# Attention whose probabilities are divided by row on GpSimd and turned by a transpose, with neighbourhood values in matmuls of 512 columns

## The reference, cut to what matters

```python
# kind A: every query sees all 1024 keys; 8 query heads share 2 key/value heads
sc = jnp.einsum('bqkgd,bskd->bkgqs', qi, k).astype(jnp.float32) * scale
p = jax.nn.softmax(sc, axis=-1)
o = jnp.einsum('bkgqs,bskd->bqkgd', p, v)
# kind B: tokens form a grid of 16 rows x 64 columns; a query sees 8 rows x 16 columns
r0 = jnp.clip(r - kh // 2, 0, rows - kh)
sc = jnp.where(mask, sc + bias, -jnp.inf)     # learned bias by relative position
p = jax.nn.softmax(sc, axis=(-2, -1))
o = jnp.einsum('bhjqkc,bkjchd->bjqhd', p, v_band)
```

## Time and profile before

| | |
|---|---|
| median of 3 runs | 2989.11 us (2982.98 to 2990.6) |
| span of the profiled execution, first to last instruction | 2980.2 us; its own time is not recorded apart from the span |
| TensorE busy | 2780.2 us, 93% |
| VectorE / ScalarE / GpSimd busy | 1447.7 / 923.2 / 161.8 us |
| mean granted TensorE clock | 0.965 |
| attention, kind A | about 2376 to 2633 us of the span |
| attention, kind B | about 2633 to 2862 us of the span |

### The profile page before, as it was taken

The page is one execution under the profiler, slowest core; times in us unless marked ns, Lnnn a source line. Parts: engine busy times, 40 slices in busy tenths (PEclk is TensorE's granted clock), DMA queues, the critical chain, the costliest instruction groups (busy, mean ns, idle before and its releaser), DMA issues.

```text
span 2980.2 us, 36559 instructions
## 1 busy us (share of the span) xinstructions
PE 2780.2 (93%) x13564; PEld 2272.1 (76%) x13564; DVE 1447.7 (49%) x2275; ACT 923.2 (31%) x1437; POOL 161.8 (5%) x128
## 2 busy tenths in 40 slices
PE   8989999999997999989999999999999999988988
PEld 2467777777776988867787787777788888877876
DVE  3764444454436144244434334345412188877753
ACT  3342222222123222242222222223212266654531
POOL 2100000000002000100000000000100000022111
PEclk9999999999998998999999999999999999999888
DMA  8522222222102600221111111102434522233311
GB/s 301 184 67 80 93 84 84 84 84 85 57 15 81 177 8 21 93 99 56 43 42 43 56 42 42 42 0 106 122 114 143 134 58 65 81 92 102 84 71 57
DMA packets 179482, 245.34 MB, mean 82 GB/s; under 512 B 55728, under 2 KB 136752, under 8 KB 179376
## 3 DMA queue, kind: packets, MB, share of 16 engines
q1 hardware_dynamic: 156944, 208.52, 21.6%
q10 hardware_dynamic: 22432, 35.40, 4.4%
HBM read 210.33 MB, written 39.58 MB: 84 GB/s over the span
## 4 chain that ended last, share of the span: by engine, by line
PE 79%; issue 7%; DVE 7%; ACT 4%; DMA 1%; POOL 1%; ACTq 1%; DVEq 0%; SPq 0%; POOLq 0%
PE banks L1615 20%; PE banks L1616 19%; PE banks L1617 19%; PE banks L1961 5%; PE banks L1695 3%; PE banks L1990 2%; DVE Hlo L1286 1%; ACT Whi L842 1%; PE banks L1979 1%; PE banks L1802 1%; PE banks L1803 1%; PE banks L1804 1%; PE banks L1948 1%; DVE X L1331 1%; PE banks L1949 1%
## 5 line engine op out<-in xcount | busy, mean ns | idle before, releaser
L1615 PE MATMUL banks<-Hhi,Whi 128*128 128x512 f32 x1792 | 714.2, 399 | 17.4 <-ACT TB L964 6.7
L1616 PE MATMUL banks<-Hlo,Whi 128*128 128x512 f32 x1792 | 703.6, 393 | 0.0
L1617 PE MATMUL banks<-Hhi,Wlo 128*128 128x512 f32 x1792 | 703.3, 392 | 0.0
L1331 DVE SCALAR_TENSOR_TENSOR X<-banks,mod,X 128x512 f32<-128x512 f32 x512 | 373.4, 748 | 243.2 <-PE banks L1617 243.2
L1615 PE MATMUL banks<-Mhi,Whi 128*128 128x512 f32 x1024 | 411.4, 402 | 58.9 <-DVE X L1331 58.9
L1615 PEld LDWEIGHTS banks<-Hhi,Whi 128*128 128x128 f32 x1792 | 341.1, 190 | 97.5 <-issue 8.7
L1616 PE MATMUL banks<-Mlo,Whi 128*128 128x512 f32 x1024 | 404.9, 395 | 0.0
L1617 PE MATMUL banks<-Mhi,Wlo 128*128 128x512 f32 x1024 | 404.7, 395 | 0.0
L1616 PEld LDWEIGHTS banks<-Hlo,Whi 128*128 128x128 f32 x1792 | 340.8, 190 | 74.0 <-issue 4.2
L1617 PEld LDWEIGHTS banks<-Hhi,Wlo 128*128 128x128 f32 x1792 | 340.1, 190 | 72.0
L842 ACT ACTIVATE Whi<-stage 128x2048 fp32r<-128x2048 f32 x93 | 177.3, 1907 | 636.1 <-PE banks L1617 622.6
(11 more groups left out here) (171 smaller groups left out, 3032.4 us busy)
## 6 DMA issues: line engine op xcount, KB each, us to landing
stage<-w SPq DMA_DIRECT2D x64, 1024.0 KB, 5.6
stage<-ada_w SPq DMA_DIRECT2D x48, 1024.0 KB, 5.2
stage<-w_in SPq DMA_DIRECT2D x13, 1024.0 KB, 6.5
stage<-sgu_in SPq DMA_DIRECT2D x8, 1024.0 KB, 6.8
x_saved<-X SPq DMA_DIRECT2D x16, 512.0 KB, 2.7
X<-x_saved SPq DMA_DIRECT2D x16, 512.0 KB, 6.1
QS<-q_heads ACTq DMA_DIRECT2D x28, 256.0 KB, 3.9
KH<-k_heads ACTq DMA_DIRECT2D x28, 256.0 KB, 3.9
```

What stands on the lines that cost most here:

```text
L1331: nc.vector.scalar_tensor_tensor(out=X[:, k, half(hf)], in0=Dn[:, i % D_BANKS, :], scalar=gate[:, k:k + 1], in1=X[:, k, half(hf)], op0=ALU ...
L1615: nc.tensor.matmul(out_bank, whi, xhi, start=start, stop=False)
L1616: nc.tensor.matmul(out_bank, whi, xlo, start=False, stop=False)
L1617: return nc.tensor.matmul(out_bank, wlo, xhi, start=False, stop=stop)
```

## The change

It is confined to the attention of the second block, and has four parts.

1. The division by the row sum leaves the turn. GpSimd multiplies the row of probabilities in place by the reciprocal (`scale`, a `tensor_scalar` with the reciprocal as a per-partition scalar). VectorE no longer makes the diagonal matrix. The turn becomes `nc.tensor.transpose`, a matmul in transpose mode against the identity, and waits for `scale` instead of the diagonal.
2. The value product of kind B takes whole groups as that of kind A does: the turned probabilities are stored at their place among all key tiles, the group's six key tiles are multiplied in 512 columns, and what no query of the group sees there is zero. The zeros are written once per buffer by GpSimd (`zero_window`, `zero_pad`) since nothing overwrites them. Outputs of a group start when all four units' turned probabilities are there.
3. The mask is added to the bias table in two halves, for the first head of a pair during units 13 and 14 of the pair before, for the second head at units 4 and 5.
4. Loads are issued from SyncE's queue in the order of need, each as soon as its buffer is free, not from ScalarE's at set units.

```diff
@@ helpers @@
+    def probs_t(x, u, kind, k, m):
+        k += neighbourhood(u % QT)[0] // 2 if kind == "B" else 0
         return x[:, (u // 4) % 2, k:k + m, (u % 4) * P:(u % 4 + 1) * P]
+    def key_tiles(kind, g):
+        return range(KT) if kind == "A" else range(2 * (g % 2), 2 * (g % 2) + 6)
@@ SyncE @@
+            def attend(T, kind, i, before, last):
+                following = ("B", 0) if last else (kind, i + 1)
+                if before is not None:
+                    for what in ("q", "kh", "kl", "bias", "v"):
+                        if what in needed(kind):
+                            load_head(sync, T, kind, i, 1, what)
+                if not (last and kind == "B"):
+                    for what in ("q", "kh", "kl", "bias", "v"):
+                        if what in needed(following[0]):
+                            load_head(sync, T, *following, 0, what, ahead=1)
@@ GpSimd @@
-            def mask_bias(T, e):
-                pool.wait_ge(mask_loaded, 16)
-                pool.wait_ge(bias_loaded[e], T.loads(16, 4))
-                nc.gpsimd.tensor_tensor(bias[:, e, :], bias[:, e, :], mask[:], ALU.add).then_inc(bias_masked, 1)
+            def scale(T, u, kind):
+                pool.wait_ge(rd_done, T("v", u + 1))
+                pool.sem_inc(sums_seen, 1)
+                row = PE_[:, u % 2, 0:width(kind, u)]
+                nc.gpsimd.tensor_scalar(out=row, in0=row, scalar1=rden[:, u % 4:u % 4 + 1], scalar2=1.0,
+                                        op0=ALU.mult, op1=ALU.mult).then_inc(probs_scaled, 1)
+            def mask_bias(T, e, part, ahead=0):
+                if part == 0:
+                    pool.wait_ge(mask_loaded, 16)
+                    pool.wait_ge(bias_loaded[e], T.loads(16, 4, ahead))
+                at = slice(part * (NF + NI) // 2, (part + 1) * (NF + NI) // 2)
+                nc.gpsimd.tensor_tensor(bias[:, e, at], bias[:, e, at], mask[:, at], ALU.add).then_inc(bias_masked, 1)
+            def zero_pad(T, u):
+                reach(pool, t_ready, T("v2", 2 * u - 2))
+                nc.gpsimd.memset(PE_[:, u % 2, NI:NI + HD], 0.0).then_inc(pad_zeroed, 1)
+            def zero_window(T, g):
+                reach(pool, o_ready, T("vg", g - 1))
+                outside = (((4, 6, 0, 256), (5, 6, 256, 384), (0, 1, 384, 512)),
+                           ((2, 4, 256, 512), (7, 8, 0, 128), (2, 3, 128, 256)))[g]
+                for x in (PTh, PTl):
+                    for k0, k1, q0, q1 in outside:
+                        nc.gpsimd.memset(x[:, g, k0:k1, q0:q1].bitcast(F32), 0.0).then_inc(window_zeroed, 1)
             def attend(T, kind, i, before, last):
                 for u in range(PAIR):
-                    if kind == "B" and u in (0, 4):
-                        reach(pool, mixed_done, T("vg", u // 4 - 2))
-                        mask_bias(T, u // 4)
-                    if kind == "B" and u in (3, 7):
-                        pool.wait_ge(bias_masked, T.masked(u // 4))
+                    if u % 4 == 0:
+                        reach(pool, mixed_done, T("vg", (u - 5) // 4))
+                    for w, k in lagged(u, 2, kind, before):
+                        scale(T, w, k)
+                    if kind == "B" and before == "A" and u < 2:
+                        zero_pad(T, u)
+                    if kind == "B" and before == "A" and u in (4, 8):
+                        zero_window(T, u // 4 - 1)
+                    if kind == "B" and u in (4, 5):
+                        mask_bias(T, 1, u - 4)
+                    if (kind == "B") != last and u in (13, 14):
+                        mask_bias(T, 0, u - 13, ahead=1)
                     for w, k in lagged(u, 8, kind, before):
                         if w % 4 == 3:
+                            pool.wait_ge(probs_scaled, T("v", u - 1))
                             gated(T, w // 4, tile_of(kind, i, w < 0))
@@ VectorE, invert_sum @@
-                reach(dve, rd_done, T("v", u - 3))
-                nc.vector.reciprocal(rden[:, u % 4:u % 4 + 1], den[:, u % 4:u % 4 + 1]).then_inc(rd_own, 1)
-                dve.wait_ge(rd_own, T("v", u + 1))
-                reach(dve, t_ready, T("v2", 2 * u - 2))
-                nc.vector.tensor_scalar(out=DG[:, u % 2, :], in0=con("ident"), scalar1=rden[:, u % 4:u % 4 + 1],
-                                        scalar2=None, op0=ALU.mult).then_inc(rd_done, 1)
+                reach(dve, probs_scaled, T("v", u - 3))
+                nc.vector.reciprocal(rden[:, u % 4:u % 4 + 1], den[:, u % 4:u % 4 + 1]).then_inc(rd_done, 1)
@@ TensorE, turn @@
-                pe.wait_ge(rd_done, T("v", u + 1))
+                pe.wait_ge(probs_scaled, T("v", u + 1))
                     reach(pe, tl_done, T("v2", 2 * u + g - 1))
                     for k in range(m):
                         a = (first + k) * P
-                        part = min(P, n - a)
-                        ins = nc.tensor.matmul(TP[0:part, g, k * P:(k + 1) * P], PE_[:, u % 2, a:a + part],
-                                               DG[:, u % 2, :], start=True, stop=True)
+                        ins = nc.tensor.transpose(TP[:, g, k * P:(k + 1) * P], PE_[:, u % 2, a:a + P], con("ident"))
@@ TensorE, outputs @@
+                    pe.wait_ge(tl_done, T("v2", 8 * g + 8))
+                tiles = key_tiles(kind, g)
+                todo = [(k, x) for k in tiles for x in (PTh, PTl)]
+                n = len(todo) // 4
+                for k, x in todo[n * part_of:n * part_of + n]:
+                    ins = nc.tensor.matmul(OB[:, g % 2, :], VT[:, e, k, :], x[:, g % 2, k, :],
+                                           start=k == tiles[0] and x is PTh, stop=k == tiles[-1] and x is PTl)
```

More of the change, by code:

```diff
@@ L73 @@
          "finish").split()
-LOAD_AT = {1: "q", 2: "kh", 3: "kl", 4: "bias", 7: "v"}
 class Tally:
@@ L1084, in exp, with probs_hi @@
                                      accum_out=den[:, u % 4:u % 4 + 1]).then_inc(exp_done, 1)
-            def probs_hi(T, u, n):
-                for g, first, m in banks(n):
+            def probs_hi(T, u, kind):
+                for g, first, m in banks(width(kind, u)):
                     act.wait_ge(t_ready, T("v2", 2 * u + g + 1))
@@ L1100, in attend @@
             def attend(T, kind, i, before, last):
-                following = ("B", 0) if last else (kind, i + 1)
                 for u in range(PAIR):
                     for w, k in lagged(u, 3, kind, before):
-                        probs_hi(T, w, width(k, w))
-                    if before is not None and u in LOAD_AT and LOAD_AT[u] in needed(kind):
-                        load_head(nc.scalar, T, kind, i, 1, LOAD_AT[u])
-                    if u - QT in LOAD_AT and not (last and kind == "B") and LOAD_AT[u - QT] in needed(following[0]):
-                        load_head(nc.scalar, T, *following, 0, LOAD_AT[u - QT], ahead=1)
+                        probs_hi(T, w, k)
                     for w, k in lagged(u, 1, kind, before):
@@ L1950, in scores, with turn @@
                 ins.then_inc(s_ready, 1)
-            def turn(T, u, n):
-                pe.wait_ge(rd_done, T("v", u + 1))
-                for g, first, m in banks(n):
+            def turn(T, u, kind, zeroed=0):
+                pe.wait_ge(probs_scaled, T("v", u + 1))
+                reach(pe, pad_zeroed, zeroed)
+                for g, first, m in banks(width(kind, u)):
                     reach(pe, tl_done, T("v2", 2 * u + g - 1))
@@ L1973, in outputs @@
                     reach(pe, os_done, T("vg", g - 1))
-                if kind == "A":
-                    if part_of == 0:
-                        pe.wait_ge(tl_done, T("v2", 8 * g + 8))
-                    for k in (2 * part_of, 2 * part_of + 1):
-                        for x in (PTh, PTl):
-                            ins = nc.tensor.matmul(OB[:, g % 2, :], VT[:, e, k, :], x[:, g % 2, k, :],
-                                                   start=k == 0 and x is PTh, stop=k == QT - 1 and x is PTl)
-                else:
-                    pe.wait_ge(tl_done, T("v2", 2 * w + 2))
-                    t = part_of
-                    first, rows = neighbourhood(w % QT)
-                    n = rows * GRID
-                    tiles = (n + P - 1) // P
-                    for k in range(tiles):
-                        part = min(P, n - k * P)
-                        for x in (PTh, PTl):
-                            ins = nc.tensor.matmul(OB[:, g % 2, t * P:(t + 1) * P],
-                                                   VT[0:part, e, first // 2 + k, :],
-                                                   x[0:part, g % 2, k, t * P:(t + 1) * P],
-                                                   start=k == 0 and x is PTh, stop=k == tiles - 1 and x is PTl)
+                    pe.wait_ge(tl_done, T("v2", 8 * g + 8))
+                    reach(pe, window_zeroed, zeroed)
+                tiles = key_tiles(kind, g)
[4 more added lines that the diff above has]
```

(5 more changed lines are left out.)

40 lines of the change are left out of this document (22 added, 18 removed).

## The result

The changed kernel takes 2866.3 us in the median of 4 runs (2865.0 to 2869.0), the kernel before 2986.1 us beside it on the same chip (2980.7 to 2990.6). The ratio is 0.960, with a 95% interval of 0.9584 to 0.9617: 120 us less. The forecast was 2911 us, 78 less, in a range of 2872 to 2968. The profiled execution spans 2867.1 us (2980.2 before).

The account below looks back on a forecast made before the run. TensorE was taken to bound the attention, with VectorE right behind in A. A -37, B -50, clock +13 and tail -4 sum to -78 us: span 2902, time 2911 us, range 2872 to 2968 for 8 in 10.

Parts of the forecast that it names:

- TensorE bounds A, and a transpose is one pass at the same pace: Kind A's turn: one 0.111 us pass per transpose instead of two, so TensorE needs 2.72 us a unit, not 3.61.
- The rival of a transpose without gain: Turn on TensorE: transpose no cheaper than two passes, only the stall goes in A; about 2950 us; 8 in 100.
- the circles: Waits closing every two units: in A 3.5 us plus scale via GpSimd, 5.2 via VectorE; scale under 1.9 us is covered.
- the midpoint to the two-input row: Scale on GpSimd: half the two-input slope, 1.06 ns a column plus 0.2 us; 1.29 us in A, 0.78 in B.
- what goes and what comes at a group's end: End of four units: vanished stall of 1 us mostly taken back by 0.8 us in A, 0.7 in B.
- The stalls: VectorE's diagonal beside GpSimd's gating multiply lasts 1.30 us, not 0.29; 34 us over all 128 diagonals.
- The new wait behind the gating product: Group ends: gating multiply (1.28 us) sits before the next scale on GpSimd's queue, adding 0.8 us in A, 0.7 in B.
- the allowances for limits that lie close: Unit times: A taken at 2.9 us with TensorE at 2.72; B at 2.3 with limits near 1.8 to 1.9.
- the loads, "mostly beside waits: nothing": Load issues leaving ScalarE's queue, about 1.1 us per pair, mostly beside waits: costed at nothing.
- the clock, +13 us: Kind B: TensorE less busy, so more lower clock; a quarter of units at 3.6 us instead of 2.8, 13 us added.
- this rival's event: Clock falls to the lower level in A too, +86 us there if throughout, 3075 us; 8 in 100, half of it mild.
- Tail: After the last units: 12 matmuls of 0.43 us and a 2 us wait replace 46 small ones of 10.86 us; -4 us.

Follow-up runs that it names:

- cut gating product: Kernel before with GpSimd's gating product cut to 8 of 512 columns, leaving most of that product out: 2944.2 us, ratio 0.988.
- the one with small outputs: Changed kernel with kind B's value product again in 128 columns for each unit: 2898.8 us, ratio 0.973.

## Why the prediction was off in size, step by step

**Right: TensorE bounds A, and a transpose is one pass at the same pace.** 0.110 us for 0.111, a unit at 2.71 for 2.72. The rival of a transpose without gain is ruled out.

**Right: the circles.** The scale took 1.119 us where 1.29 were worked out, and at 512 and 576 columns 0.692 and 0.745 for 0.78: 0.83 ns a column and some 0.27 us fixed, so the memset row was its near relative, not the midpoint to the two-input row. It hides either way.
**Right: what goes and what comes at a group's end.** The stalls were computed at 34 us. The cut gating product takes out those beside it and leaves those beside the masks: the diagonals are busy 49.8 us instead of 70.7, and the time falls by 37. In A that is 0.75 us a group for a stretch of 1.0; in B, at 1.56, it brings the clock with it. The new wait behind the gating product was put at 0.8 and 0.7 us a group; moving it away gives 0.85 and 0.82.

**Wrong: the allowances for limits that lie close, 0.2 us a unit in A and 0.4 in B.** "For two limits so close I allow 0.2 and take 2.9." In the trace after there is no such jitter: TensorE's 2.71 and VectorE's 2.66 run beside each other, and a group of A takes 4 x 2.71 + 1.83 = 12.67 instead of 13.7. Over 16 groups of A that is 16 us, 12 of them the allowance and 4 the group's end, 1.8 for 2.1 (at A's start and end the steps are uneven, so A as a whole lies 15 below). In B the limits were put near 1.9 us and 2.3 was taken. In three groups at full clock (turns from 2639.88, 2650.15 and 2660.24 us on) the turns follow at 1.6 to 2.1 us, 1.9 in the mean, so the limit was right and the allowance was not there. The group's end costs some 2.5 us for 2.0. With the clock's part a group was foreseen at 11.2 + 0.8 = 12.0 and took 10.25.

These allowances and the clock below are the steps that failed. Of the 35 us between the forecast 78 and the spans' 113, 15 lie in A and 21 in B with its tail, 13 of which were put on the clock; the remaining 7 of the medians' 120 are the difference between spans and medians.

**Wrong: the loads, "mostly beside waits: nothing".** Moving them was worth 30 us in the kernel before (the end of the waits for the bias included) and, put back, they cost 32 in the kernel after. ScalarE's queue is in order, and the issues stood behind a copy and ahead of an exponential that two circles wait for: about 1.1 us each time, in view in the chain of before. This isn't a second gap in the sum: the sum builds a group from the limits of the units, in which no issue stands, so the loads' gain was in it without being named. The error lies in the reading. Had the loads stayed, half of A's allowance would have been needed: put back, they raise a group of A by 0.38 us, 0.1 a unit.

**Wrong in sign: the clock, +13 us.** The prediction read the lower level as a matter of how little TensorE does in B and expected more of it. TensorE does do less, 135 us busy in 175 after 207 in 229, yet the granted clock of B rose from 0.89 to 0.96. In the kernel before, stand in stretches that begin behind gaps; each edit that shortens gaps, the cut gating product alone or the loads alone, brings B to 1.00 with the matmuls unchanged. With the wide outputs the falls in the kernel after are over in 3.4 us; in the kernel before they held for 3.4 us twice, for 13.7 twice, and for over 14 at the end of B. So the 13 us were not there, and part of the low stretches of before went as well.

**The other rivals.** The clock did not fall in A: 1.00. With the scale doubled it does, for 3.4 us at a time behind longer idle times of TensorE, so gaps can bring this rival's event, in small. The Trainium skill's page TensorE: Matmul & The Clock Gate, Part 4, says that transpose mode doesn't count as busy. No run here bears that out for float32: 400 transposes with nothing else for 43.9 us keep 1.00. The measurement decides; the chance of 8 in 100 rested on no row.

**Tail.** Forecast -4. The step from the last but two to the last gating product fell from 19.9 to 11.0 us, -9. The chain after has 12 wide products in 3.00 us, 0.25 each:

```profile
2744.56 0.43 DVE PTl L1596
...
2745.13 3.00 PE banks L2019 x12
```

The prediction had them at 0.43, the lower level.

**The parts against the whole.** Undone one at a time, the pass, the masks, the loads and the wide outputs give 59, 38, 32 and 38 us, 167 for a whole of 120 (148 by the bare medians), and the stalls are not among them. The lower clock is charged to most of the undoings: B's clock is 0.88, 0.90 and 0.83 in three of the four. It is one likely reason for the excess; another is that the scale on GpSimd makes whole masks and late reciprocals dearer than they were before. How B's 62 us divide between shorter work and clock stays open.

## What to carry to other kernels

Count every DMA issue as work on the in-order queue that issues it, and look in the chain of waits whether it stands ahead of an operation that others wait for; moving loads to an idle queue was worth 1% here. Where gaps lower TensorE's clock, an edit that closes a gap can pay twice, and its undoing be charged twice, so gains measured one by one need not add up. Where two limits lie close, take the larger one for the forecast and put the slack into the range, not into the sum. When a helper engine takes a short, urgent step into its queue, move its long, patient steps one slot behind the urgent one: here that was another 20 us.

## What the runs showed of the hardware

- The weight load of a float32 transpose is recorded with 140 ns, that of a two-pass float32 matmul of equal size with 192; from start to start both have 0.11 us.
- Multiplying by a scalar per partition on GpSimd takes 1119, 745 and 692 ns for 128 x 1024, 576 and 512 float32, in place.
- With 128-column products in B the lower clock, once reached, held for 3.4 us in some cases and for 13.7, 17 and 24 us in others (the kernel before and the one with small outputs); with 512-column ones the falls were of 3.4 us, and up to 6.9 in the kernel with whole masks.
- Beside the two-input gating product on GpSimd VectorE's 128 x 128 multiplication by a scalar per partition takes 1.30 us instead of 0.29, and the row maximum of a PSUM bank its usual 1.21.
- The bias load takes 8.0 us to land when SyncE issues it behind the other loads of its pair, 4.2 when ScalarE issued it at a unit of its own.
